# A conv / sparse-attention block in fp32: the value chunks of the convolution in another matmul form

## The reference

```python
def conformer_conv(h, w_in, dw, dw_b, ln_g, ln_b, w_out):
    u = h @ w_in
    a, b, z = jnp.split(u, 3, axis=-1)
    v = a * jax.nn.sigmoid(b)
    pad = CONV_WIDTH // 2
    v = lax.conv_general_dilated(
        v, dw[:, None, :].astype(v.dtype), window_strides=(1,), padding=[(pad, pad)],
        dimension_numbers=("NWC", "WIO", "NWC"), feature_group_count=WIDTH) + dw_b
    v = jax.nn.silu(layer_norm(v, ln_g, ln_b))
    return (v * jax.nn.silu(z)) @ w_out
```

## Time and profile before

| | |
|---|---|
| median of 3 runs | 2467.63 us (2464.0 to 2469.48) |
| profiled execution, its own time | 2469.33 us |
| its span in the profile | 2467.6 us |
| TensorE busy | 2344.5 us (95%) |
| VectorE, ScalarE, GpSimd busy | 1580.9, 1271.6, 226.5 us |
| convolution, from first matmul of the chunks to the projection out | some 20 to 320 us |

### The profile page before, as it was taken

One profiled execution on the slowest core, in us unless ns is written; L12 is line 12 of the kernel. 1 busy time (PEld: TensorE's weight loads), 2 busy tenths in 40 slices (PEclk: granted clock), 3 DMA queues, 4 the chain that ended last, 5 costly groups with the idle time before them and its releaser, 6 DMA issues.

```text
span 2467.6 us, 37399 instructions
## 1 busy us (share of the span) xinstructions
PE 2344.5 (95%) x14290; PEld 2075.8 (84%) x14290; DVE 1580.9 (64%) x2311; ACT 1271.6 (52%) x1383; POOL 226.5 (9%) x53
## 2 busy tenths in 40 slices
PE   6999988999999999989899988977999999999999
PEld 6999977888888888878788867867888888888888
DVE  6777766677666676666566665654556555655566
ACT  6555554666666665445566675444344334433333
POOL 4777720000000000000000000000000000000000
PEclk9999999999999999999999988988999999999999
DMA  5444444444444443545444422531455555555556
GB/s 220 171 171 174 174 164 163 171 165 168 154 154 156 156 162 108 203 146 215 156 149 153 153 86 76 183 133 69 171 187 188 189 187 187 188 189 190 191 194 221
DMA packets 57426, 409.45 MB, mean 166 GB/s; under 512 B 6496, under 2 KB 6624, under 8 KB 8544
## 3 DMA queue, kind: packets, MB, share of 16 engines
q1 hardware_dynamic: 57312, 407.82, 45.4%
HBM read 405.70 MB, written 2.10 MB: 165 GB/s over the span
## 4 chain that ended last, share of the span: by engine, by line
PE 88%; ACT 4%; DVE 4%; issue 3%; DMA 1%; SPq 0%; DVEq 0%; ACTq 0%
PE G L347 23%; PE G L346 23%; PE G L345 11%; PE G L348 11%; PE G L354 4%; PE G L356 4%; PE G L355 4%; DMA RAW<-stream_dram 1%; ACT HI L323 1%; PE A L977 1%; DVE LO L330 1%; PE A L964 1%; PE A L1004 1%; DVE HN L454 0%; PE A L979 0%
## 5 line engine op out<-in xcount | busy, mean ns | idle before, releaser
L323 ACT ACTIVATE HI<-RAW 128x2048 fp32r<-128x2048 f32 x381 | 728.1, 1913 | 848.1 <-DMA RAW<-stream_dram 847.2
L330 DVE TENSOR_TENSOR LO<-RAW,HI 128x2048 fp32r<-128x2048 f32 x332 | 760.2, 2290 | 325.4 <-ACT HI L323 323.7
L347 PE MATMUL G<-HX,HI 128*128 128x512 f32 x2056 | 834.1, 406 | 44.6 <-DVE HX L473 20.7
L346 PE MATMUL G<-HX,HI 128*128 128x512 f32 x2056 | 819.9, 399 | 0.0
L345 PE MATMUL G<-HX,LO 128*128 128x256 f32 x2056 | 576.9, 281 | 0.0
L348 PE MATMUL G<-HX,LO 128*128 128x256 f32 x2056 | 575.2, 280 | 0.0
L345 PEld LDWEIGHTS G<-HX,LO 128*128 128x128 f32 x2056 | 390.6, 190 | 95.2
L348 PEld LDWEIGHTS G<-HX,LO 128*128 128x128 f32 x2056 | 392.0, 191 | 86.5
L347 PEld LDWEIGHTS G<-HX,HI 128*128 128x128 f32 x2056 | 395.5, 192 | 52.9 <-DVE HX L473 22.3
L346 PEld LDWEIGHTS G<-HX,HI 128*128 128x128 f32 x2056 | 389.8, 190 | 0.0
L337 POOL TENSOR_TENSOR LO<-RAW,HI 128x2048 fp32r<-128x2048 f32 x49 | 226.3, 4619 | 100.3 <-ACT HI L323 99.9
(11 more groups left out here) (347 smaller groups left out, 2559.0 us busy)
## 6 DMA issues: line engine op xcount, KB each, us to landing
RAW<-stream_dram SPq DMA_DIRECT2D x381, 1024.0 KB, 4.8
X<-x_dram SPq DMA_DIRECT2D x4, 512.0 KB, 5.2
MB<-mem_dram SPq DMA_DIRECT2D x4, 512.0 KB, 5.5
out_dram<-X SPq DMA_DIRECT2D x4, 512.0 KB, 7.7
CON<-constants_dram SPq DMA_DIRECT2D x1, 981.0 KB, 16.4
VEC<-vectors_dram SPq DMA_DIRECT2D x1, 623.5 KB, 17.4
VEC<-vectors_dram SPq DMA_DIRECT2D x1, 272.0 KB, 7.0
CON<-constants_dram SPq DMA_DIRECT2D x1, 64.5 KB, 1.9
```

Source lines behind the costliest of these rows:

```text
L323: nc.scalar.activation(HI[:, c.slot(RING), :], RAW[:, c.slot(RING), :], ACT.Copy).then_inc(hi_ready, 1)
L330: nc.vector.tensor_tensor(LO[:, c.slot(RING), :], RAW[:, c.slot(RING), :], HI[:, c.slot(RING), :].bitcast(F32), ALU.subtract).then_inc(lo_ ...
L346: return nc.tensor.matmul(res, wh, both[:, k, :, :], start=False, stop=last)
L347: nc.tensor.matmul(res, wh, both[:, k, :, :], start=first, stop=False)
```

## The change

The value chunks (m = 1) use `product` in place of `product3`. Their result has two halves. VectorE adds them with `evict` straight into the padded tile VP, waits for its own instruction, and multiplies VP with SG in place; that instruction now raises `cv_pad`, and the bank of G is given free by the reduction. ScalarE's first taps, and the guard of SG, wait on `cv_pad`. Since `cv_pad` then counts 16 more, the later use of the same semaphore in the gating counts from `3 + KT + g`. Gate and z chunks stay as they were.

```diff
@@ -375,7 +375,7 @@
                     mm = product3(gres(r), c, k, both, k, k == 0, k == kt - 1)
             mm.then_inc(mm_done, 1)
 
-        def gemm_two(pe, c, r, h, paired=True, operand=None, lag=0):
+        def gemm_two(pe, c, r, h, paired=(True, True), operand=None, lag=0):
 
             both = HX if operand is None else operand
             groups = FILL[h]
@@ -389,7 +389,7 @@
                         wait(pe, lo_ready, c + m + 1)
                         wait(pe, g_free[(r + m).slot(NG)], (r + m).turn(NG))
                     for k in range(*groups[g]):
-                        if paired:
+                        if paired[m]:
                             mm = product(halves(r + m), c + m, k, both, k, k == 0, k == KT - 1)
                         else:
                             mm = product3(gres(r + m), c + m, k, both, k, k == 0, k == KT - 1)
@@ -676,7 +676,7 @@
 
         def conv_pe(pe):
             def project(ft, m, within=None):
-                gemm(pe, conv_chunk(ft, m), conv_result(ft, m), paired=False, within=within)
+                gemm(pe, conv_chunk(ft, m), conv_result(ft, m), paired=(m == 1), within=within)
 
             def sums(ft):
                 return (8, lambda pe: conv_sums(pe, At(ft))) if ft >= 0 else None
@@ -686,7 +686,7 @@
                     project(ft, 0, sums(ft - 2))
                     project(ft, 1)
                 else:
-                    gemm_two(pe, conv_chunk(0, 0), conv_result(0, 0), H_CONV, False, lag=2)
+                    gemm_two(pe, conv_chunk(0, 0), conv_result(0, 0), H_CONV, (False, True), lag=2)
                 if z_after(ft) is not None:
                     project(z_after(ft), 2)
             for n, z in enumerate(range(KT - Z_LATE, KT)):
@@ -722,7 +722,7 @@
             def first_taps(ft):
 
                 wait(act, cv_dw, ft + 1)
-                taken(act, conv_result(ft, 1))
+                wait(act, cv_pad, 3 + ft)
                 wait(act, cv_done, ft - 1)
                 for k in range(SUMS):
                     ins = nc.scalar.activation(tap_sum(At(ft), k), VP[:, ft % 2, k:k + T], ACT.Identity,
@@ -740,7 +740,7 @@
                 wait(act, cv_tap0, ft - 1)
                 wait(act, mm_done, c + 1)
                 if ft >= 2:
-                    taken(act, conv_result(ft - 2, 1))
+                    wait(act, cv_pad, 3 + ft - 2)
                 nc.scalar.activation(SG[:, ft % 2, :], gres(r), ACT.Sigmoid).then_inc(g_free[r.slot(NG)], 1)
                 first = V_AT["dw"] + ft * TAPS
                 nc.scalar.activation(DW[:, ft % 2, 0:SUMS], VEC[:, first:first + SUMS], ACT.Copy)
@@ -772,7 +772,7 @@
 
             def high(g):
                 k0, k1 = TWOS[g]
-                act.wait_ge(cv_pad, 3 + g)
+                act.wait_ge(cv_pad, 3 + KT + g)
                 nc.scalar.activation(HXB[:, k0:k1, 0, :], gated_tile(k0, k1).rearrange("p (k t) -> p k t", t=T), ACT.Copy).then_inc(cv_hh, 1)
 
             activate(0)
@@ -815,8 +815,10 @@
                 taken(dve, conv_result(ft, 0))
                 wait(dve, mm_done, c + 2)
                 r = conv_result(ft, 1)
-                nc.vector.tensor_tensor(VP[:, ft % 2, PAD:PAD + T], gres(r), SG[:, ft % 2, :],
-                                        ALU.mult).then_inc(g_free[r.slot(NG)], 1)
+                v = VP[:, ft % 2, PAD:PAD + T]
+                evict(dve, c + 1, r, v)
+                taken(dve, r)
+                nc.vector.tensor_tensor(v, v, SG[:, ft % 2, :], ALU.mult).then_inc(cv_pad, 1)
                 wait(dve, cv_tap0, ft + 1)
                 taps(SUMS, TAPS)
                 st.wait(st.n)
```

## The result

The changed kernel takes 2485.74 us (median of 4 runs, 2483.88 to 2490.05), the kernel before 2467.61 us (4 runs). The ratio is 1.0075, with a 95% interval of 1.0062 to 1.0087: 18 us slower. The profiled execution has a span of 2482.1 us.

A forecast was written before the change was run, and what follows sets the result against it. TensorE was taken as the bound, busy every microsecond of the convolution from 60 to 300 us. Terms -3.0 + 14.4 + 4.5 = +15.9 us on a median of 2467.63 gave 2484 us, range 2475.5 to 2491.5.

The forecast's parts named there:

- Matmul form: Convolution's value chunks on TensorE: two matmuls per slice instead of three save 3.0 us, 1.5 by the slower row.
- Exclusion: VectorE's two-SBUF-operand multiply waits for the rest of a GpSimd instruction, up to 4.62 us, plus 0.28.
- Self-feeding lateness: From tile 1, a blocked multiply makes VectorE 1.5 us late next round, so that multiply is blocked too.
- TensorE's waits: TensorE waits 4.8 us for ScalarE's square after value chunks 4, 8 and 12: three times, 14.4 us.
- the way out: Clock loss delays value chunks; VectorE catches up, slips ahead of GpSimd, skips the next stall: two stalls, no tail, +10.6 us.
- The clock: TensorE at the lower clock behind each wait: 1.6 to 2 us lost each, three making +21 or +22 in all.
- The end of the stage: Convolution's end: the sums of tile 15 wait for its late square, 4.5 us more, all of it counting.
- The bank of G: Bank released 0.27 us later by VectorE, but TensorE wants it one chunk (5.8 us) later: costs nothing.
- Rivals 1 and 2: Multiply beside GpSimd: first, not excluded, about 2465 us, chance 0.11; second, only slowed, about 2466 us, chance 0.05.
- The third: Of the rivals: two-matmul slices keep the pitch of three, multiply not excluded; 2467 to 2468 us, chance 0.02.

The follow-up runs named there:

- e1: Changed kernel, but the reduction writes its sum into PSUM, so the multiply has one SBUF and one PSUM operand: 2465.5 us, ratio 0.9993.
- e7: Changed kernel, but GpSimd takes each LO chunk in two instructions of 1024 columns instead of one of 2048: 2466.49 us, ratio 0.9997.
- e3: Changed kernel, but in feature tiles 1, 2, 5, 9 and 13 the sum goes through PSUM; the other 11 stay in place: 2465.79 us, ratio 0.9992.
- e6: As e3, but tile 9 goes back to the in-place multiply of two SBUF operands: 2473.56 us, ratio 1.0025.
- e2: Changed kernel, but value chunks again use three matmuls; VectorE copies the result into the padded tile and multiplies in place: 2488.42 us, ratio 1.0088.
- e4: Changed kernel, but ScalarE takes the square of the tile before ahead of the first taps, not behind them: 2474.16 us, ratio 1.0032.

## Why the prediction was right, step by step

The forecast was 2484 us with a range of 2475.5 to 2491.5; 2485.7 was measured. The mechanism was as forecast. The sum was right to 2 us, but its terms were not all so, and errors in them cancel. In the profiled execution, against -3.0 + 14.4 + 4.5:

- **Matmul form**: -3.0 us forecast. The sums of tile 14 (L699) start at 291.75 in e1 and at 295.37 before: -3.6. The size is about right. The other 0.6 or so comes in before tile 0: in e1 its value chunk ends about 1 us earlier than before, of which 0.18 is its own saving. What sets that in the start-up I did not follow.
- **Exclusion**: 0.28 us behind GpSimd's end, as L829 showed. L831, which is L829 under its new number, found GpSimd at rest this time and took 0.42 us. The Trainium skill ("SBUF — State Buffer", Who interferes with whom) has it that a VectorE instruction with two SBUF inputs contends with a GpSimd instruction that reads SBUF, and that the ports they share are an exclusive lock. The ends at 55.55 and 128.70, e1 and e7 all agree with that.
- **Self-feeding lateness**: a late multiply was put at V + 6.0 and the next round 1.5 us late; the blocked rounds are 18.1 to 18.2 us apart (69.67, 87.87, 106.00) with multiplies of 4 us. e3 and e6 show the mechanism by itself.
- **TensorE's waits**: three of 4.8 us forecast, two of 5.3 and 5.15 measured. The third, near 250 us, did not come, so this term of the sum was 4 us too high. TensorE escaped it by the way out that the prediction named under the clock: after the second wait V came late enough that tile 9's multiply slipped in 0.44 us ahead of GpSimd. After the first wait tile 5's missed this by 0.21 us. The prediction had expected no late end of the stage in that case. It came all the same, since tile 13 starts a series of its own. Which of the two happens behind a wait is a matter of tenths of a microsecond, and e2 recovers the other way round, behind its first wait (tiles 5 to 8) and not behind its second.
- **The clock**: left out of the sum, 1.6 to 2 us each in the range. The sums of tile 14 are 15.2 us later than in e1, of which the waits are 10.45; the rest is 4.8 us. Of that, 0.3 is there ahead of the first wait (the sums of tile 3 start at 105.86, in e1 at 105.59). From there to the sums of tile 4 it is 25.15 us instead of e1's 18.05, 1.8 more than the wait of 5.30; from the sums of tile 7 to those of tile 8 it is 25.89 instead of 18.06, 2.7 more than the wait of 5.15. That is half of the 3.6 and of the 5.6 us at the lower level. The first lies in the range given, the second above it, and the sum had neither.
- **The end of the stage**: 4.5 forecast, 7.0 measured. The wait at L699 is 4.71, and another 2.1 us come behind it until 342.86 (24.42 us against 22.34): the sums at the lower clock (2.11 us instead of 1.06 until VectorE takes over), and 1.47 us of ScalarE's wait for a weight chunk whose transfer starts only when TensorE has got past its late sums, less the 0.53 that L829 lost before. The transfer I had cost at nothing.
- Together: -3.6 + 10.45 + 4.8 + 4.9 + 2.1 = 18.6, the 18.5 us by which the projection out is late (4.9 is what the sums of tile 15 lose more than those of tile 14). That this lies within 3 us of the forecast 15.9 is partly luck: the waits in the middle came to 4 us less than forecast, the clock that the sum left out to some 4.5 more, and the end to 2.5 more.
- **The bank of G**, costed at nothing: right for the changed kernel, wrong for late rounds as such, as the two waits of 2.5 us in e4 show.

Rivals 1 and 2 fall with the multiplies of 4 us. The third does too: the two-matmul slices run at 0.35 us in the value chunks.

## What to carry to other kernels

Before giving a VectorE instruction two SBUF operands beside a busy GpSimd, look at how long one GpSimd instruction is: that, not its own 0.4 us, is what it can cost, and putting one operand into PSUM or cutting GpSimd's instruction in two takes it away. Busy shares don't show this: VectorE had a quarter of its time free. Look for the round that is late by the order of the work, ask whether its delay ends before the next one begins, and then for the instruction that stands behind it in a third engine's queue.

## What I had not expected of the hardware

The two waits of TensorE, of 5.30 and 5.15 us, cost 7.1 and 7.8 us (e6, with one of 5.29, lies 7.8 us above e3). The 1.8 and 2.7 us more come with the lower clock level behind them. It lasted 3.6 us the first time and 5.6 us the second, longer than the 3 us that I had read behind a wait of the same length in another stage. And VectorE gets its turn between two GpSimd instructions issued back to back, so that halving GpSimd's instruction took away the whole loss, at no cost that could be measured.
